# A hybrid attention and convolution block on eight cores: positions loaded first, VectorE's queue of the prologue reordered, and the squares of the attention's side jobs queued one step later

## What is computed

```python
h = rmsnorm(x, norm_g)
z = h @ w_in              # q_a 512, kv_a 256, k_pe 64, gate_a 2048, conv B, C, x, gate_c 1024 each,
                          # merge_a 2048, merge_c 2048
q = rmsnorm(q_a) @ w_uq   # 16 heads x (128 + 64); k_nope, v = rmsnorm(kv_a) @ w_ukv, 16 x (128 + 128)
q, k = rmsnorm per head (192), then the rotary tables cos, sin of the positions on the last 64
attn = softmax(q k^T / sqrt(192)) v              # bidirectional, all 2048 keys
ya = (attn * silu(gate_a)) @ w_branch_attn
yc = (B * conv3(C * xin) * silu(gate_c)) @ w_branch_conv
x = x + (sigmoid(merge_a) * ya + sigmoid(merge_c) * yc) @ w_out
x = x + sigmoid(rmsnorm(x) @ w_ple_gate) * (p @ w_ple_proj)
```

## Time and profile before

| what | value |
|---|---|
| median of 3 runs | 1657.86 us (1656.66 to 1659.07) |
| the profiled execution's own time | 1650.8 us |
| its span (slowest core) | 1649.3 us (cores: 1644.9 to 1649.3) |
| TensorE busy | 1566.0 us, 95% |
| VectorE busy | 785.7 us, 48% |
| ScalarE busy | 741.0 us, 45% |
| TensorE weight loads (beside matmuls) | 736.5 us |
| GpSimd busy | 98.3 us |
| mean granted TensorE clock | 0.988 to 0.993 over the cores |
| DMA moved | 119.02 MB |

### The profile page before, as it was taken

The page is one execution under the profiler, slowest core; times in us unless marked ns, Lnnn a source line. Parts: engine busy times, 40 slices in busy tenths (PEclk is TensorE's granted clock), DMA queues, the critical chain, the costliest instruction groups (busy, mean ns, idle before and its releaser), DMA issues.

```text
span 1649.3 us, 22791 instructions; the slowest of 8 cores (1644.9 to 1649.3 us)
## 1 busy us (share of the span) xinstructions
PE 1566.0 (95%) x7678; PEld 736.5 (45%) x7678; DVE 785.7 (48%) x1048; ACT 741.0 (45%) x1236; POOL 98.3 (6%) x181
## 2 busy tenths in 40 slices
PE   4889999999999999999999999999999999999998
PEld 1334544444444444445444444444444444444444
DVE  4783476766666765776766111111111111243555
ACT  3472578687677777787775211010110101243211
POOL 0010000000000000000000110100100110100000
PEclk8899999999999999999999999999999999999999
DMA  9762221202111210221012683444544544985511
GB/s 249 181 160 36 36 39 33 39 11 36 32 21 20 39 33 7 39 33 20 14 27 35 116 148 55 72 75 78 84 68 72 90 71 82 208 180 87 128 64 71
DMA packets 38609, 119.02 MB, mean 72 GB/s; under 512 B 4064, under 2 KB 4448, under 8 KB 37472
## 3 DMA queue, kind: packets, MB, share of 16 engines
q0 software_dynamic: 25488, 82.85, 30.3%
q1 hardware_dynamic: 13008, 34.72, 6.5%
HBM read 192.00 MB, written 8.39 MB: 122 GB/s over the span
## 4 chain that ended last, share of the span: by engine, by line
PE 85%; DVE 5%; ACT 5%; issue 3%; DMA 1%; DVEq 0%; ACTq 0%; SPq 0%
PE ps_o L908 5%; PE ps_s L848 5%; PE ps_s L850 5%; PE ps_o L966 3%; PE ps_s L969 3%; PE ps_s L1005 3%; PE ps_a L975 3%; PE ps_o L969 3%; PE ps_s L975 3%; PE ps_s L947 3%; PE ps_s L966 3%; PE ps_s L1037 3%; PE ps_s L434 2%; PE ps_a L769 2%; PE ps_a L1037 2%
## 5 line engine op out<-in xcount | busy, mean ns | idle before, releaser
L855 ACT ACTIVATE arena<-ps_s,arena 128x512 bf16<-128x512 f32 x512 | 323.6, 686 | 49.9 <-PE ps_s L850 42.9
L895 DVE TENSOR_TENSOR arena<-arena 128x1024 f32<-128x1024 f32 x224 | 273.1, 1219 | 24.0 <-ACT arena L855 18.1
L848 PE MATMUL ps_s<-arena 128*128 128x512 bf16 x512 | 194.5, 380 | 9.5 <-ACT arena L855 9.0
L850 PE MATMUL ps_s<-arena 128*128 128x512 bf16 x512 | 194.5, 380 | 0.0
L908 PE MATMUL ps_o<-arena 128*128 128x512 bf16 x512 | 152.7, 380 | 1.2 <-ACT arena L911 1.2
L848 PEld LDWEIGHTS ps_s<-arena 128*128 128x128 bf16 x512 | 50.1, 98 | 77.8 <-issue 20.7
L850 PEld LDWEIGHTS ps_s<-arena 128*128 128x128 bf16 x512 | 50.1, 98 | 57.9 <-issue 0.7
L978 ACT ACTIVATE arena<-ps_o 128x512 f32<-128x512 f32 x16 | 9.6, 597 | 129.3 <-PE ps_o L966 129.3
L908 PEld LDWEIGHTS ps_o<-arena 128*128 128x128 bf16 x512 | 49.5, 98 | 39.3 <-issue 2.2
L980 DVE SCALAR_TENSOR_TENSOR arena<-arena,ps_s 128x512 f32<-128x512 f32 x16 | 11.0, 688 | 115.7 <-PE ps_s L972 115.7
L980 DVE SCALAR_TENSOR_TENSOR arena<-arena,ps_b 128x512 f32<-128x512 f32 x16 | 11.0, 688 | 115.3 <-PE ps_b L972 115.3
(11 more groups left out here) (280 smaller groups left out, 2587.2 us busy)
## 6 DMA issues: line engine op xcount, KB each, us to landing
arena<-w_dense POOLq DMA_DIRECT2D x48, 512.0 KB, 5.8
arena<-w_merge POOLq DMA_DIRECT2D x48, 512.0 KB, 6.0
arena<-x_fm SPq DMA_DIRECT2D x16, 1024.0 KB, 8.3
arena<-w_pg POOLq DMA_DIRECT2D x16, 576.0 KB, 6.2
arena<-x_fm SPq DMA_DIRECT2D x16, 512.0 KB, 19.7
arena<-w_out POOLq DMA_DIRECT2D x16, 512.0 KB, 7.3
out<-arena SPq DMA_DIRECT2D x31, 256.0 KB, 2.0
arena<-w_q POOLq DMA_DIRECT2D x16, 256.0 KB, 3.5
```

Of the source, the lines that this page charges most:

```text
L848: P.op("pe", lambda h, bk=bk, qs=qs: h.matmul(bk.ap, lhsT=Kb.ap[:, kt * 128:(kt + 1) * 128], rhs=Qa.ap[:, qs], start=True, stop=False), re ...
L850: P.op("pe", lambda h, bk=bk, qs=qs: h.matmul(bk.ap, lhsT=KrT.ap[:, kt * 128:(kt + 1) * 128], rhs=Qb.ap[:, qs], start=False, stop=True), r ...
L855: P.op("act", lambda h, sb=sb, qb=qb: h.activation(out=pt.ap[:, qb * 512:(qb + 1) * 512], in_=sb.ap, func=AF.Exp, scale=so.ap[:, kt:kt + 1 ...
L895: P.op("dve", lambda h, pt=pt, ac=ac: h.tensor_tensor(out=ac.ap, in0=ac.ap, in1=pt.ap, op=ALU.add), reads=R(ac, *pt.rl), writes=R(ac))
```

## The change

On the side of the loads and the tables:

```diff
         half = []
+        for i in range(2):
+            ld("sp", posrow[i].ap, pos_d[:, 1024 * i:1024 * i + 1024], posrow[i], P.slot(f"pos{i}"))
         for q in range(4):
             ld("pool", WlK.ap[:, 4 * q:4 * q + 4, :], w_latk_d[:, 4 * q:4 * q + 4, :], WlK.rl[q], P.slot(f"wk{q}"))
-        load_x(0, 8, range(2))
-        ld("sp", posrow[0].ap, pos_d[:, 0:1024], posrow[0], P.slot("pos0"))
-        load_x(0, 8, range(2, 8))
+        load_x(0, 8)
...
-        ld("sp", posrow[1].ap, pos_d[:, 1024:2048], posrow[1], P.slot("pos1"))
```

In the loops of the prologue:

```diff
+        tabs = [table(TABa, posrow[0]), table(TABb, posrow[1])]
+        steps(4)
         mm = lat(0, WlK, 3, kbanks[0])
         for j in range(8):
             A_sq(0, j)
             A_x(0, 2 * j)
             A_x(0, 2 * j + 1)
-            if j > 1:
-                next(tab)
-            if j > 4:
-                next(tab)
+            if j == 0:
+                steps(4)
+            elif j == 1:
+                steps(7)
+                sine(TABa)
+            elif j == 3:
+                steps(2)
+                sine(TABb)
             go(mm, 6 * j, 6 * j + 6)
             A_ss(0, j)
-        for _ in tab:
-            pass
         A_rs(0)
-        sine(TABa)
-        e1_sq(0)
```

In the attention:

```diff
+        owed = {}
+
+        def off(b, fn):
+
+            def once():
+                if owed.get(id(b)) is once:
+                    del owed[id(b)]
+                    fn()
+            owed[id(b)] = once
+            later(once)
+
         def take():
             b = [b_ for b_ in rota if b_ is not held[0]][0]
+            if id(b) in owed:
+                owed[id(b)]()
...
-            P.op("act", lambda h: h.activation(out=sq.ap, in_=bk.ap, func=AF.Square), reads=R(bk), writes=R(sq))
+            off(bk, lambda: P.op("act", lambda h: h.activation(out=sq.ap, in_=bk.ap, func=AF.Square), reads=R(bk), writes=R(sq)))
...
-            P.op("act", lambda h: h.activation(out=sqA.ap, in_=rawn.ap, func=AF.Square), reads=R(rawn), writes=R(sqA))
+            later(lambda: P.op("act", lambda h: h.activation(out=sqA.ap, in_=rawn.ap, func=AF.Square), reads=R(rawn), writes=R(sqA)))
...
-            P.op("act", lambda h: h.activation(out=sqB.ap, in_=bk.ap, func=AF.Square), reads=R(bk), writes=R(sqB))
+            off(bk, lambda: P.op("act", lambda h: h.activation(out=sqB.ap, in_=bk.ap, func=AF.Square), reads=R(bk), writes=R(sqB)))
...
-                for qb, (s1, s2, s3) in enumerate(((5, 7, 9), (10, 11, 12))):
+                for qb, (s1, s2, s3) in enumerate(((5, 7, 9), (10, 11, 13))):
...
-                    for v_, s_ in enumerate((7, 8, 9, 12, 13, 14, 15)):
+                    for v_, s_ in enumerate((7, 8, 9, 12, 12, 14, 15)):
```

More of the change, by code:

```diff
@@ L498, in go, with steps @@
                 f()
-        tab = table(TABa, posrow[0])
-        P.op("act", lambda h: h.activation(out=rq.ap[:, 0:1], in_=col(COL_EPS), func=AF.Ln), reads=R(cols), writes=R(rq))
+        tabs = [table(TABa, posrow[0]), table(TABb, posrow[1])]
+        def steps(n):
+            for _ in range(n):
+                if next(tabs[0], None) is None:
+                    next(tabs[1], None)
+        steps(4)
         mm = lat(0, WlK, 3, kbanks[0])
@@ L525, in build_nc @@
             A_x(1, 2 * j + 1)
-            if j == 2:
-                e1_mm(0, banks[3])
+            if j == 3:
+                e1_scale(0)
+                e1_sq(0)
             elif j == 4:
+                e1_rope(0)
+            elif j == 5:
+                fin = e1_mm(0, banks[3])
+            elif j == 6:
                 e1_ss(0, banks[3])
-            elif j == 5:
+            elif j == 7:
                 e1_cmb(0)
-            if j != 2:
-                A_b(0, j if j < 2 else j - 1)
+            if j in (5, 6, 7):
+                A_b(0, j - 5)
             go(mm, 6 * j, 6 * j + 6)
             A_ss(1, j)
+        fin()
         A_rs(1)
-        for c in range(7, 11):
+        for c in range(3, 6):
             A_b(0, c)
+        e1_scale(1)
         e1_sq(1)
-        for c in range(11, 16):
+        for c in range(6, 8):
+            A_b(0, c)
+        e1_rope(1)
+        for c in range(8, 13):
+            A_b(0, c)
+        mm = lat(0, WlQ, 4, qbanks[0])
+        go(mm, 0, 28)
+        fin = e1_mm(1)
+        go(mm, 28, 36)
+        e1_ss(1)
+        for c in range(13, 16):
             A_b(0, c)
         load_x(2)
-        mm = lat(0, WlQ, 4, qbanks[0])
-        go(mm, 0, 12)
-        e1_mm(1)
-        go(mm, 12, 20)
-        e1_ss(1)
-        go(mm, 20, 28)
-        e1_cmb(1)
+        fin()
         for c in range(16):
@@ L558, in build_nc @@
         mm = [m4[4 * kc + m] for kc in range(16) for m in range(3)] + m4[3::4]
[L559 to L561 removed]
+        go(mm, 0, 12)
+        e2_mm(0)()
+        go(mm, 12, 20)
         for j in range(8):
@@ L584, in build_nc @@
         mm = lat(2, WlK, 3, kbanks[2])
-        go(mm, 0, 5)
-        e2_mm(1)
-        go(mm, 5, 14)
+        go(mm, 0, 9)
+        fin = e2_mm(1)
+        halo(2)
+        fin()
+        go(mm, 9, 16)
         for j in range(8):
@@ L591, in build_nc @@
             A_x(3, 2 * j + 1)
-            if j == 1:
-                sine(TABb)
-            go(mm, 14 + 4 * j, 14 + 4 * j + 4)
-        go(mm, 46, 48)
+            go(mm, 16 + 4 * j, 16 + 4 * j + 4)
+        A_rs(3)
+        e1_scale(2)
         e1_sq(2)
-        A_rs(3)
+        e1_rope(2)
         halo(3)
-        run(lat(3, WlK, 3, kbanks[3]), ins(*e1_ins(2)))
+        mm = lat(3, WlK, 3, kbanks[3])
+        go(mm, 0, 18)
+        e1_mm(2)()
+        go(mm, 18, 30)
+        e1_ss(2)
+        go(mm, 30, 36)
+        e1_cmb(2)
+        go(mm, 36, 48)
+        e1_scale(3)
         e1_sq(3)
+        e1_rope(3)
         AT = mk(32896, BF16, [16, 1024], "AT")
@@ L828, in build_nc @@
         first = [lambda tb=tb: jK(0, tb) for tb in range(3)]
-        first.insert(1, lambda: e1_mm(3))
+        first.insert(1, lambda: later(e1_mm(3)))
         first.insert(3, lambda: e1_ss(3))
         first.append(lambda: e1_cmb(3))
-        for qb in range(2):
-            first += [lambda qb=qb: jQn(0, qb), lambda qb=qb: jQr(0, qb), lambda qb=qb: jQs(0, qb)]
-        first += [lambda: jK(0, 3), lambda: jV(0, 0), lambda: jKc(0)]
+        first += [lambda: jQn(0, 0), lambda: jQr(0, 0), lambda: jK(0, 3), lambda: jQs(0, 0)]
+        first += [lambda: jQn(0, 1), lambda: jQr(0, 1), lambda: jV(0, 0), lambda: jQs(0, 1), lambda: jKc(0)]
         first += [lambda v_=v_: jV(0, v_) for v_ in range(1, 8)]
```

80 lines of the change are left out of this document (38 added, 42 removed).

## The result

The changed kernel takes 1683.5 us in the median against 1658.1: ratio 1.0149, interval 1.0132 to 1.0167. In some executions one die runs at a much lower mean clock (one of the five here took 1909.3 us), and the ratios are of the others alone. It is slower by 1.5%; 1664 was forecast.

What follows compares the result with a forecast made beforehand. TensorE was taken to bound every stage, with only its idle gaps to win or lose. Prologue -5 and -5.8, heads' start -3, attention +22 gave +8, taken as +6: 1664 us in the median's terms, range 1654 to 1676.

Steps and rivals of the forecast that it cites:

- Block 0's end: Prologue, first half: block 0 ends at 42.5 us where it ended at 36.25, 6 us lost.
- block 1's: Prologue, first half: block 1 starts at once and ends at 60.8 to 62 us, where it ended at 66.25.
- the first half: First half of the latent projections, blocks 0 and 1: 5 us won, 3 to 7.
- the second half: Second half of the latent projections: table loads and waits go, 63.2 us left of 68.95, 5.8 won (3 to 7).
- the start of the heads: Ahead of the attention: Qs gets a job between itself and its squares, 3 us won (1 to 4).
- near 59: Sign in the attention: TensorE's idle time, 37.7 us before, would come near 59 us.
- The 24 early writers: Attention: 24 jobs in a bank just left wait 1.8 us each for its late square, 43 us.
- Rival 1: Attention: shared banks cost as little as today, early waits average under 1.5 us, whole kernel 1628 us; 22%.
- the scores and jQs: Attention, step 12: waits behind ACT's squares go with squares a step later and Qs in step 13, -15 us.
- The taps: Attention: three convolution taps no longer together on VectorE, which held the longest wait; -1 us.
- rival 2: Prologue gives nothing: TensorE stays at 1.2 GHz through block 0 into block 1, about 10 us lost, 1674; 13%.
- The last move: Whole sum: +8 us taken as +6, since two stalls in one step overlap in part.

Runs made afterwards that it cites:

- the spread table: Changed kernel with jK's and jQr's squares in place, plus the second sine table's eight instructions spread over block 0's chunks: 0.9811 of the kernel before.
- the second measurement: The changed kernel with no edit, timed again on the chip of a later run against the kernel before: ratio 1.0100.
- the kernel with one extra square: The kernel with the spread table, plus one matmul in step 14 of 15 heads waiting for one added ScalarE square: 1.0058 of the kernel before.

## Why the prediction was wrong

The sign was right and most steps held; the size was short: +25 us measured in those runs, +6 forecast, outside the range by 3.5. The 19 us between them are some 7 of clock behind the new waits, which the sum did not have, 2 that I had taken off it, and 9 or so that only the first chip showed and whose cause is open.

**The prologue: right, in part by two errors that cancel.** Block 0's end was put at 42.5 and came at 42.9; block 1's at 60.8 to 62 and came at 63.9 on core 1, where PE ran at 0.81 or less between 42.7 and 58 us, and at 60.9 and 62.1 on cores 4 and 7. So the first half gained 2.4 on this core (5 forecast, 3 at least), the second half 7.0 (5.8 forecast, 69.1 us down to 62.2), the start of the heads 4.0 (3). The first score matmul is 13.3 us earlier, 13.8 was the sum. Block 0 ended 6.6 us later than before, 6 as said, and the spread table won 4.7 of them back there. ACT's table loads ahead of the heads are two, where I named three, each followed at once by its activation (17.08, then 18.38; 43.15, then 44.44), with no drain behind them.

**The attention's idle time: right, and closer than its terms.** 22 us more was the sum, 22.2 is measured; "near 59" was 59.4. The 24 early writers, followed through take() and hold(), are the 24 waits in the trace, at 1.8 each in the forecast and 43 us together in both. Undoing the two `off` lines takes them away, and each line alone takes its own. Rival 1 (waits under 1.5 us on average) fell: 1.79. But the match to 0.2 us is luck: the scores and jQs fell from 15.9 to 2.5 us, 13.4 where I had 15, and all other waits rose from 21.3 to 56.9, by 35.6 where I had 37. The taps were off by more, 1 us in the sum and 4 in the run.

**The step that failed** is one that the sum never had: the clock in the attention. I read 1.00 in the earlier trace rows for that stage and carried it over, although the change puts 24 new waits there and the earlier trace rows show cold matmuls behind a gap. The busy time rose by 7 us on cores without the stretches at 0.81 (684.5 of 743.9 us on core 7), in five stretches at half clock; the longest waits (2.85, 2.95, 3.17 us) each had one behind them, and so did two 1.62 us waits of jKc, whose own matmuls are one column wide. Over the eight cores 23 of the 24 waits near 3 us had one, 14 of the 56 of jKc at 1.6, and none of the 112 others at 1.5 to 1.9. In the forecast's words, rival 2 priced the clock in the prologue, where it cost little, and nobody priced it behind the waits. With +22 and +7 against -13 the sum is +16, and the second measurement gives +16.5.

That term alone leaves the time at 1674, inside the range. What took it out is the slower die: its core 1 was busy for 11 us more in the attention than core 7, and 3 more in the tail, in the stretches at 0.81. The second measurement of the same kernel has none of it; whether the program or that chip calls it forth stays open.

**The last move** was wrong too: I shaded +8 to +6 because two stalls in one step might overlap. The idle time shows nothing of it. The three waits near 3 us are not two of PE's stalls either, but places where ACT had more ahead of the square than the exponentials: at 242.07 and 856.90 a read of the dense bank (L838) that itself stood 2.13 us behind DVE, at 817.92 two more instructions (L789, L790).

## What to carry to other kernels

Before a read is moved to a later place in an engine's queue, ask who needs the thing it releases, not only who needs its result: here the square's result had a step to spare, but its bank was the next job's. Price every new wait of the bounding engine twice, once as idle time and once for the clock behind it, here 2 us for each wait of 4.4, and a stretch at half clock behind 23 of 24 waits near 3. And look which long instruction stands ahead of the short reads that free a buffer: moving one 1.22 us sum behind them won 21 us, nearly as much as this whole change wins with jK's and jQr's squares in place (24).

## What the runs showed of the hardware that was not expected

A wait of TensorE of 4.4 us in the middle of dense work cost 2.0 us more in lower clock, the mean over 15 of them; waits of 1.6 us that stood alone, ahead of 512-column matmuls, cost none, on any core. The same wait in the same execution can cost clock on one core and none on another: in the kernel with one extra square the wait of 2.94 us left the clock at 1.00 on core 2 and not on core 0, so a rule by length alone would be wrong. The same file ran with one die of a chip at a granted clock of 0.81 for stretches of 15 us, its slowest core 14 to 18 us behind the other die's in each of the four runs that count there, while on the chip of the later run both dies were alike within 4 us.
